# The first tile's last gathered row in another buffer, and seven instead of four of the second tile's last rows summed by TensorE

## The reference

```python
scores = einsum('bshcd,hckd->bshck', q, sub_keys)        # 8 heads, 2 halves, 128 keys
s_top, i_top = lax.top_k(scores, 16)
best, pos = lax.top_k(all 16x16 sums of the two halves, 16)
expert_idx = i_top[first] * 128 + i_top[second]          # of 16384 experts
u = jnp.take(expert_u, ic, axis=0)                       # 8 KB a row
act = gelu(einsum('ckd,cd->ck', u, xc))
vv = jnp.take(expert_v, ic, axis=0)
y = einsum('ck,ckd->cd', gate * act, vv)                 # 128 rows a token
out = rms_norm(h + y, final_norm)
```

## Time and profile before

| | |
|---|---|
| median of 3 runs | 2009.05 us (2001.18 to 2010.74) |
| profiled execution, its own time | 2006.39 us |
| its span in the trace | 2004.2 us |
| TensorE (PE) busy | 1847.6 us, 92% |
| VectorE (DVE) busy | 1389.4 us, 69% |
| ScalarE (ACT) busy | 599.3 us, 30% |
| GpSimd (POOL) busy | 958.6 us, 48% |
| DMA moved | 633.76 MB, mean 316 GB/s |

### The profile page before, as it was taken

How to read it: one execution, slowest core, us unless ns; L and a number is a source line. 1 busy time by engine, 2 the same in 40 slices (tenths; PEclk the granted TensorE clock), 3 DMA queues, 4 the chain that set the end, 5 groups by cost and what they waited for, 6 DMA issues and landing times. The chain is left out here.

```text
span 2004.2 us, 20780 instructions
## 1 busy us (share of the span) xinstructions
PE 1847.6 (92%) x6862; PEld 1212.0 (60%) x6863; DVE 1389.4 (69%) x2403; ACT 599.3 (30%) x1085; POOL 958.6 (48%) x643
## 2 busy tenths in 40 slices
PE   7999999999999999798888878989888999999986
PEld 6888888888888898654545434444434554444432
DVE  5464453223334338898898887989889978888977
ACT  5445463345543520121111132333315620000001
POOL 4443343444332413564554566666655645444462
PEclk9999999999999999899888999999998999999997
DMA  8976464555554679999999999999999979999997
GB/s 212 246 171 148 136 192 156 190 192 186 168 168 163 209 248 387 359 405 414 415 419 411 416 417 403 404 409 397 416 397 393 402 304 416 413 411 378 398 368 310
DMA packets 159381, 633.76 MB, mean 316 GB/s; under 512 B 29291, under 2 KB 34483, under 8 KB 98995
## 3 DMA queue, kind: packets, MB, share of 16 engines
q0 software_dynamic: 73728, 424.74, 52.7%
q1 hardware_dynamic: 85552, 207.74, 32.1%
HBM read 742.49 MB, written 2.10 MB: 372 GB/s over the span
## 5 line engine op out<-in xcount | busy, mean ns | idle before, releaser
L578 POOL TENSOR_TENSOR w_lo<-raw,w_hi 128x1024 fp32r<-128x1024 f32 x112 | 273.5, 2442 | 425.4 <-ACT w_hi L703 425.0
L1694 PE MATMUL acc<-w_hi,t_hi 128*128 128x512 f32 x896 | 354.9, 396 | 0.0
L1696 PE MATMUL acc<-w_hi,t_lo 128*128 128x512 f32 x896 | 349.2, 390 | 0.0
L1695 PE MATMUL acc<-w_lo,t_hi 128*128 128x512 f32 x896 | 348.7, 389 | 0.0
L1076 DVE TENSOR_TENSOR w_lo<-raw,w_hi 128x1024 fp32r<-128x1024 f32 x112 | 152.5, 1361 | 263.6 <-ACT w_hi L703 263.5
L703 ACT ACTIVATE w_hi<-raw 128x1024 fp32r<-128x1024 f32 x224 | 237.0, 1059 | 328.3 <-PE acc L1696 296.2
L620 POOL DMA_INDIRECT u_ring<-in_peer_u_dram,idx x160 | 198.7, 1242 | 249.8 <-DVE dots L1518 175.7
L1514 DVE CUSTOM_DVE_ANT_0 junk<-u_ring,hn 128x1024 bf16<-128x1024 f32 x160 | 195.8, 1224 | 47.5 <-DMA u_ring<-in_peer_u_dram,idx 39.9
L2043 PE MATMUL misc<-v_low,diag 128*128 128x512 f32 x408 | 203.5, 649 | 25.4 <-DMA v_low<-in_peer_v_dram,idx 23.5
L1518 DVE CUSTOM_DVE_ANT_0 junk<-u_ring,hn 128x1024 bf16<-128x1024 f32 x160 | 195.2, 1220 | 0.0
L1696 PEld LDWEIGHTS acc<-w_hi,t_lo 128*128 128x128 f32 x896 | 168.2, 188 | 35.6
(11 more groups left out here) (318 smaller groups left out, 2716.3 us busy)
## 6 DMA issues: line engine op xcount, KB each, us to landing
u_ring<-in_peer_v_dram SPq DMA_DIRECT2D x48, 1024.0 KB, 8.8
raw<-in_w_in_dram SPq DMA_DIRECT2D x64, 512.0 KB, 5.9
raw<-in_xattn_wk_dram SPq DMA_DIRECT2D x32, 512.0 KB, 5.1
raw<-in_xattn_wv_dram SPq DMA_DIRECT2D x32, 512.0 KB, 3.9
raw<-in_w_out_dram SPq DMA_DIRECT2D x32, 512.0 KB, 4.6
raw<-in_xattn_wq_dram SPq DMA_DIRECT2D x32, 512.0 KB, 4.7
raw<-in_xattn_wo_dram SPq DMA_DIRECT2D x32, 512.0 KB, 4.8
praw<-in_peer_wq_dram SPq DMA_DIRECT2D x24, 512.0 KB, 8.1
```

The source lines that it names most:

```text
L578: nc.gpsimd.tensor_tensor(w_lo[:, j % RING, :, :], raw[:, j % RING, :, :], w_hi[:, j % RING, :, :].bitcast(F32), ALU.subtract).then_inc(lo ...
L1694: nc.tensor.matmul(o, xh, w_hi[:, s, kk, :], start=first, stop=False)
L1695: nc.tensor.matmul(o, xh, w_lo[:, s, kk, :], start=False, stop=False)
L1696: ins = nc.tensor.matmul(o, xl, w_hi[:, s, kk, :], start=False, stop=last)
```

## The change

The order of buffers for the first tile's rows is turned so that row 127 lies in buffer 5 instead of buffer 0; `PE_ROWS` begins at row 104 instead of 113, so it has seven rows (104, 107, 110, 113, 116, 119, 122) and not four; ScalarE writes all of their diagonals but the last ahead of the first tile's squares and scaling.

```diff
@@ def v_index(n): @@
             if n < WIDE_V[0]:
                 return (0, 1, 6, 7)[n % 4]
-            return (0, 1, 4, 2, 3, 5)[(n - WIDE_V[0]) % 6] if n < WIDE_V[1] else (0, 1, 2, 3, 5)[(n - WIDE_V[1]) % 5]
+            return (0, 1, 4, 2, 5, 3)[(n - WIDE_V[0]) % 6] if n < WIDE_V[1] else (5, 0, 1, 2, 3)[(n - WIDE_V[1]) % 5]
...
-        PE_ROWS = tuple(range(LATE + 1, SHARED - 1, 3))
+        PE_ROWS = tuple(range(LATE - 8, SHARED - 1, 3))
...
-            for m in PE_ROWS[:3]:
+            for m in PE_ROWS[:-1]:
                 late_diagonal(m)
             squares_0()
             scaled(0)
-            for m in PE_ROWS[3:]:
+            for m in PE_ROWS[-1:]:
                 late_diagonal(m)
```

## The result

| | before | after |
|---|---|---|
| median | 2006.47 us (2001.18 to 2010.85, 8 runs) | 2013.47 us (2011.44 to 2016.24, 8 runs) |
| ratio, 95% interval | 1 | 1.0035 (1.0024 to 1.0047) |
| profiled execution, its own time | 2006.39 us | 2013.17 us |
| its span | 2004.2 us | 2011.0 us |

The change makes the kernel 7 us slower. That is less than 0.5%, but the interval of the ratio does not hold 1. The forecast was 2005.5 us with a range up to 2013.0; by its own sum the change was to win 2.4 us.

What follows compares the result with a forecast made beforehand. The DMA engines were taken as full from mid-kernel to the end. Of 15.1 us idle DMA won, 14 us went at row 113's wait; the last add came 2.4 us sooner, giving 2005.5 us, range 1997 to 2013.

Steps and rivals of the forecast that it cites:

- Step (e): Group 14, where the buffer orders meet: row 112's gather waits 13.3 us for TensorE's take of row 110, costed at nothing.
- step (b): Behind the dense part: row 113's gather waits for TensorE's take of row 104, going out at 1948.8, 13.4 us later.
- (c): Last fifteen rows: the 15 us won are idled away in 14 us at row 113's wait; DMA ends at 1989.5.
- (d): Kernel end: three more TensorE rows, 10.3 us; VectorE's last add decides, at 1990.8 instead of 1993.20, 2.4 us less.
- Step (a): First late rows: with row 127 in buffer 5, rows 3 to 13 are gathered from 1609; 10.1 us idle DMA goes.
- Step (f): Buffers 3 and 5 swapped in groups 8 to 13, and three more diagonals on idle ScalarE: no cost.
- Late dot products: Rival, chance 0.17: group 14's third dot-product row lands after 1525.8, delaying the dense part and everything after: 2012 to 2015 us.
- blocked gather: Rival, chance 0.08: row 14's gather is held while VectorE adds without pause, DMA dry for 20 us: 2010 to 2012 us.

Runs made afterwards that it cites:

- seam_seven: Changed kernel, still seven TensorE rows and row 127 in buffer 5, but no buffer reused after two rows where the orders meet: 2009.33 us, +1.9 against before.
- slots_only: Kernel before with the change's new buffer order alone, four TensorE rows and diagonals as before: 1999.25 us, 8.2 us under before.
- seam_four: Kernel before plus row 127 in buffer 5, without the reuse after two rows, four TensorE rows from 113: 1993.75 us, 13.7 us under before.
- seam_gate4: seam_four with TensorE's four rows 104, 116, 119 and 122, so 104 replaces 113: 2010.84 us, 2.6 us above before.
- after_diag: Changed kernel with all seven diagonals written ahead of ScalarE's squares and scaling of the first tile: 2014.72 us, 6.5 us above before.
- rows_only: Kernel before with the seven TensorE rows from 104 and their diagonals alone, on the old buffer order: 2012.71 us, 5.2 us above before.
- seam_114: seam_four with TensorE's first late row 114 instead of 113: 1993.32 us, 14.3 us under before.
- seam_seven_late: seam_four with seven TensorE rows, all from 113 on, and the change's order of diagonals: 2002.26 us, 6.0 us under before.
- seam_four_again: The kernel seam_four unchanged, measured once more in another set: 1993.4 us, 14.2 us under before.
- seam_tail4: seam_four with TensorE's four rows 119, 120, 122 and 123, so no gather waits for its late takes: 2002.08 us, 6.2 us under before.
- seam_narrow: seam_four with late rows going round nine buffers from row 90 instead of 102: 2001.15 us, 6.4 us under before.

## Why the prediction failed

**Step (e), the wait in group 14, is the one that failed.** The prediction put the wait at 13.3 us (15.06 measured) and "cost it at nothing, covered by the 20.1 us between that gather and its use". The row of that gather was indeed in time: its dot product ran at 1525.40, 0.38 us sooner than before. But the wait costs 5.1 and 5.5 us in the two pairs of kernels with and without it. The queue lay 9 us idle of 20 (0.55 against 1.00) in a stretch in which it is otherwise full, and the rows behind the first one came late. Waits of VectorE for the rows of its dot products between 1500 and 1625, after and then before:

```profile
L1514 DVE CUSTOM_DVE_ANT_0 junk<-u_ring,hn 128x1024 bf16<-128x1024 f32 x22 | 27.0, 1227 | 3.9 <-DMA u_ring<-in_peer_u_dram,idx 2.6 <-issue 0.5 <-DVE pos L1397 0.3
...
L1514 DVE CUSTOM_DVE_ANT_0 junk<-u_high,hn 128x1024 bf16<-128x1024 f32 x5 | 6.2, 1239 | 2.3 <-DMA u_high<-in_peer_u_dram,idx 1.9
```

```profile
L1514 DVE CUSTOM_DVE_ANT_0 junk<-u_ring,hn 128x1024 bf16<-128x1024 f32 x22 | 26.9, 1224 | 1.4 <-issue 0.5 <-DVE pos L1397 0.3
```

With 0.6 us for `u_mid` that is 5.1 us of waits for landings where the kernel before has none. They make the two groups 6.6 us longer and start the dense part 5.76 us later, of which 4.07 us are left from its second half on. That the dry queue, and not the wait as such, is what makes those rows late was read from the trace and not varied alone.

**The rest of the error lies behind the dense part.** The last row's add was forecast at 1990.8 and came at 2001.35, 10.55 us later, and step (e) is 4.07 us of that. In step (b) the take of row 104 was put at the end of a dense part whose last tile does not wait for its data; it waited 1.53 us (0.3 us more have no single place). GpSimd then took 3.05 us to go on, where the forecast had 0.9: 2.15 us. In steps (c) and (d) it was to be 42.0 us from the gather of row 113 to the last add, and it was 44.5: 2.47 us, for which no run names one cause (the five kernels with this gate lie between 42.8 and 44.5). seam_seven, the change without its wait in group 14, shows what these are worth together: it was to be 2.4 us faster than before and measured 1.9 us slower, and the interval of its ratio, 0.9999 to 1.002, just holds 1.

**Step (a), row 127 in buffer 5, held.** Late rows 3 to 5 go out without the 24.26 us wait, rows 6 and 7 wait 5.79 and 2.51 us, and the notch's DMA share goes from 0.58 to 0.99. slots_only shows the order to be worth 8.2 us net, and seam_four 13.7 us once the seam is mended, of the 15.1 us counted as idle. Part of this was luck. Only 10.1 of the 15.1 us lie in the notch that step (a) removes; 4.0 us lay behind the 21.48 us gather of row 103, and nothing in the prediction says why they should go. They went, because that gather took 7.13 us and the share from 1900 to 1920 rose to 1.02.

**Steps (b) and (c), the gate at row 113, held in kind.** The wait was forecast and so was the dry time (0.20 from 1940 to 1960). The wait was longer, 42.25 us and not 15 to 30, as GpSimd had reached it early, and the gate opened at 1956.88 and not at 1948.8. That the time won is idled away there is shown by seam_four and seam_gate4, which differ in one row: 16.3 us.

**Step (d), TensorE and VectorE at the end.** The wait for the diagonal of row 122, forecast at 1.4 to 2 us, was 7.53 us, as ScalarE stood 7.92 us for VectorE's reduced squares. after_diag shows that it did not count: the landing of rows did. TensorE's three more takes are hidden only because the gate leaves it waiting anyway; without the gate they cost 7.7 us.

**Step (f), at no cost.** The three more diagonals cost nothing in groups 14 and 15: rows_only, which writes them too, takes 101.0 us for the two groups, as before. The swap of buffers 3 and 5 was not run alone.

**The rivals.** "Late dot products" named the right mechanism, and its 2012 to 2015 us hold the result; it had a chance of 0.17. Its number is partly luck: its own condition, that the row of the third dot product lands late, did not come true, and its +6 us on a forecast of -2.4 would be 3.6 us slower than before, where 7.0 were measured. The sign of being wrong that the prediction named, a first dense tile later than 1622, came true. The blocked gather did not come at row 14, which took 1.00 us; its neighbours took 1.0 to 2.1 us.

The sum that the runs support: 13.7 us won by row 127 (seam_four), 5.1 to 5.5 lost at the seam and 15.2 to 15.6 at the gate, 7.0 slower. That the terms add up says nothing, since they are steps between the same kernels; what does say something is that each loss has the same size, within 0.4 us, with and without the other. Forecast were 15.1 won, 14 lost at the gate, nothing at the seam.

## What to carry to other kernels

Where a DMA queue is full, a wait of the engine that feeds it can cost time even if the consumer of the next transfer is not late: here 9 us of dry queue cost 5.1 to 5.5 us. Count dry DMA time, and not only the slack of the first user. When a buffer's reader is moved to an engine that gets to it late, look up which gather reuses that buffer and what is queued behind it: here one row (104 or 113) was worth 16 us. And where two orders of buffers meet, write out the distance of each reuse across the seam.

## What was not expected of the hardware

**A gather that is held while VectorE runs.** In each kernel that narrows at row 102 the gather of row 103, the first issued after 6.02 us of idle time of GpSimd, is the long one: 21.48 us before and in rows_only, 19.10 in seam_114, 16.70 in after_diag, 14.30 or 14.31 in seam_seven, seam_seven_late, seam_four_again and seam_gate4, 11.92 in seam_tail4, 9.52 in seam_four, 7.13 in slots_only and after. These are 9, 8, 7, 6, 5, 4 and 3 times a row's add of 2.39 us, less 0.02 to 0.04, so a hold lasts over 6 to 18 of VectorE's instructions of 1.28 us and not over one, and VectorE's first pause began within 2 us of its end. The more rows VectorE added without a pause, the longer the hold. Whether the pause is what ends it is not shown: in most of these kernels it began 0.9 us before the gather's end, but in seam_four, seam_four_again and after 1.5 to 1.6 us behind it, so that VectorE was still adding when the gather ended. The same kernel, seam_four and seam_four_again, was held 9.52 us in one trace and 14.31 in the other. seam_narrow moved it to another row (19.22 us, 8 times 2.39 and 0.10 more), so nothing in row 103 itself is the cause. Why most gathers of 1.0 to 1.3 us slip in between the same adds, and this one does not, stays open. A pause of GpSimd comes before each held gather (6.02 us, 3.50 in seam_narrow), but it is not enough: row 91 in seam_narrow was issued after 7.12 us of idle time into the same run of adds, and took 1.28 us:

```profile
1847.65 1.28 POOL L636 DMA_INDIRECT v_more<-in_peer_v_dram,idx  x1 [7.12 <-DVE y_sum L1580]
```

**GpSimd goes on late at the gate of row 113.** There it issued the gather 3.0 to 3.1 us after the take that released it had ended (after: 1953.83 to 1956.88; seam_gate4: 1952.05 to 1955.09; seam_seven: 1950.98 to 1954.02; after_diag: 1956.91 to 1959.95), against 0.8 us after the 24.26 us wait of the earlier trace rows and 0.8 us in the changed kernel's 1961.49, after the take that ended at 1960.70. These four waits were 40 to 50 us long, but the length is not the reason: in rows_only GpSimd had waited only 22.67 us, less than in the earlier trace rows, and went on 3.04 us after the take (1955.19 to 1958.23).

```profile
1951.59 3.60 PE L2052 MATMUL acc<-late_h,diag 128*128 128x512 f32 x8
```

```profile
1958.23 1.94 POOL L628 DMA_INDIRECT late_h<-in_peer_v_dram,idx  x1 [22.67 <-DVE y_sum L1572]
```
